# Down projections of the two MLPs: one 512-column stream past the high weights in place of two 256-column streams

## The chip, the cores and the metric

The kernel runs on one core of one Trainium2 chip. The metric is the device time of one execution in microseconds (us), as the median of several runs. TensorE (PE) does the matrix products, with a row of its own for weight loads (PEld); VectorE (DVE), ScalarE (ACT) and GpSimd (POOL) do the elementwise work; SyncE (SP) issues the weight transfers.

## The reference

A sequence of 256 tokens of width 1024 goes through two blocks of a first model (an mLSTM mixer with an MLP, then a gated short convolution with an MLP) and through one block of a second model (retention and pooling, cross attention over 256 memory rows, a gated feed-forward part, a last norm). The change touches the two MLPs of the first model alone:

```python
def sqrelu_mlp(x, w_up, w_down):        # 1024 -> 4096 -> 1024
    h = jax.nn.relu(x @ w_up)
    return (h * h) @ w_down

# in each of the two layers:
x = x + rms_norm(h, g[1])
h = sqrelu_mlp(rms_norm(x, g[2]), w_mlp_up[i], w_mlp_down[i])
x = x + rms_norm(h, g[3])
```

## The kernel before

Activations lie transposed in SBUF: 128 features per partition row, tokens along the free side (T = 256 columns). All weights reach the core as one sequence of slabs of 1 MB, each of 16 tiles of 128 x 128 (8 input chunks `k` by 2 output chunks `n`). SP loads slabs into four raw buffers. To keep the precision of fp32, each operand is split into a high part (rounded to fp32r) and a low part (the rest): ACT writes `wH` from `raw` (line 790), DVE writes `wL = raw - wH` (line 1230), each slab in two halves, into two buffers each. The `split` of slab b waits for PE to be done with slab b - 2.

For each tile PE does three products of 256 columns (`products`): high weights by high input (line 404), high weights by low input (405), low weights by high input (406). Each is a weight load and a matmul, so the high weights are loaded twice in a row. All three add up in the same 256 columns of a PSUM bank. A *triple* below is these three. Some phases (`slab_by_token`, lines 431 to 433) do the same with the operands the other way round.

A phase of the work is a run of slabs for one projection (`PHASES`, in program order, with the engine that drains each group's PSUM). Groups alternate between two PSUM tensors, `po0` and `po1`, each of two banks of 512 columns, of which 256 are used. A down projection (`down0`, `down1`) has 16 slabs in 4 groups of 4 slabs; each group gives 256 output features. Its input is the hidden activation in `hH` and `hL` (32 chunks of 256 columns each), written by ACT (line 983) and DVE (line 1491) in the up phase before it.

When a down group is done, ACT alone drains it (`keep_y`): a Square of the sum into `squares` (line 838) for the norm, then two Identity operations with the gain as scale into `y` (line 844). POOL adds up the squares of groups 0 to 2. After the last group PE goes on with a *filler*: a slab or two of work for the later cross attention (`f1` after layer 0, `f6` and `f3` after layer 1). Within the first filler slab, after chunk k = 1, PE takes the sums of squares (`norm_sums`, line 472), for which it waits for the last Square; after k = 4 it spreads the norm factors (`norm_spread`, line 479), for which it waits for DVE. DVE then scales y (line 1450), x is updated, and the next phase's inputs `xnH` and `xnL` are made; PE waits for these at the first slab of the next phase. The order on ACT at the end of a down phase is: first half of a weight split, Square, two Identities, second half of the split. That is the order in which the code is written; every engine takes its instructions in its own program order.

Of the kernel before, what the change touches and what calls it, by code (L numbers as in the profile page):

```python
# [9 lines left out]
P = 128  # L10
T = 256
# [3 lines left out]
F1 = 4 * D  # L15
# [17 lines left out]
HL = 2  # L33
# [1 line left out]

PHASES = [
# [6 lines left out]
    ("fup", 2 * F2 // 256, 2 * F2 // 256, "V"), ("fdown", F2 // P // 2, 4, "V"),  # L43
# [29 lines left out]
def build(nc, xT, memT, pos, weights, wgate, params, poolw, tri, mask, select, decay, freq, recount, out):  # L73
# [4 lines left out]
    with ctx:  # L78
        place = [nc.sbuf_base + (-nc.sbuf_base) % 64]

        def sb(name, shape, dt, at=None):
            size = int(np.prod(shape[1:])) * 4
            if at is None:
                off = place[0]
                place[0] += (size + 31) // 32 * 32
            else:
                off = at[0]
                at[0] += (size + 31) // 32 * 32
            return nc.alloc_sbuf_tensor_at(name, list(shape), dt, offset=off)

        def sem(name):
            return ctx.enter_context(nc.semaphore(name))
# [24 lines left out]
        at = [scratch]  # L117
# [19 lines left out]

        region = place[0]
        at = [region]
        hH = sb("hH", [P, F1 // P, T], f32r, at)  # L140
        hL = sb("hL", [P, F1 // P, T], f32r, at)
        hidden_end = at[0]

        cost = sb("cost", [P, T], f32, at)
# [121 lines left out]
        s_sum, s_ms, s_r, s_diag, s_R = sem("sumsq"), sem("mean_sq"), sem("r_ready"), sem("diag_ready"), sem("R_done")  # L266
        s_Rs = sem("R_kept")

        s_t, s_xadd, s_xaddV = sem("y_scaled"), sem("x_added_pool"), sem("x_added_dve")

        s_dch, s_ach, s_pch = sem("dve_chain"), sem("act_chain"), sem("pool_chain")
# [43 lines left out]
        def slot(g):  # L315
            return po[g % 2]
# [74 lines left out]
        def _(pe):  # L391
# [9 lines left out]
            def products(psum, n, w, k, aH, aL, ac, start, stop):  # L401
# [3 lines left out]
                pe.matmul(psum[:, n, 0:T], wH[w][:, wc], aL[:, ac, :], start=False, stop=False)  # L405
                return pe.matmul(psum[:, n, 0:T], wL[w][:, wc], aH[:, ac, :], start=False, stop=stop)  # L406

            def slab(s, w, psum, aH, aL, c0=0, first=True, last=True, ready=None, between={}):

                for k in range(8):  # L410
                    if k % 4 == 0:
                        weights_ready(s, k // 4)
                    if ready and k % 2 == 0:
                        pe.wait_ge(ready[0], ready[1] + k // 2 + 1)
                    for n in range(2):
                        mm = products(psum, n, w, k, aH, aL, c0 + k, first and k == 0, last and k == 7)
                    if k == 3:
                        mm.then_inc(s_half, 1)
                    if k in between:
                        between[k]()  # L420
                mm.then_inc(s_slab, 1)
# [170 lines left out]
            def mlp(layer, feed, n_norm, names):  # L592
                up, down = f"up{layer}", f"down{layer}"
                s0, g0 = SLAB0[up], GROUP0[up]
                d0 = DRAIN[g0][1]

                for j in range(4):
                    phase_slab(up, j, xnH, xnL, ready=(s_xn, 4 * feed) if j == 0 else None,
                               between=norm(n_norm) if j == 1 else {})
                with pe.Fori(0, 3) as i:  # L600
                    for j in range(4):

                        pe.wait_ge(s_drain["V"], i * 4 + (d0 + 4 + j - 2))
                        slab(i * 4 + (s0 + 4 + j), (s0 + j) % HL, slot(g0 + j), xnH, xnL)

                s0, g0 = SLAB0[down], GROUP0[down]
                d0 = DRAIN[g0][1]
                with pe.Fori(0, 2) as i:
                    for j in range(2):

                        slot_free(g0 + j)
                        pe.wait_ge(s_drain["A"], i * 2 + (d0 + j - 2))
                        for kk in range(4):
                            b = s0 + 4 * j + kk
                            slab(i * 8 + b, b % HL, slot(g0 + j), hH, hL, c0=8 * kk, first=kk == 0, last=kk == 3,
                                 ready=(s_hid, 16 * layer + 4 * kk) if j == 0 else None)
                fillers(names, n_norm + 1)

# [156 lines left out]
        def _(act):  # L775
# [60 lines left out]
            def keep_y(psum, g, gain):  # L836
# [7 lines left out]
                    k = act.activation(dst, psum[:, e, 0:T], ACT.Identity, scale=by)  # L844
                k.then_inc(s_drain["A"], 1)

            def mix_hi(src, pair, done):
                act.wait_ge(*done)
                act.activation(mixH[:, 2 * pair:2 * pair + 2, :], src, ACT.Copy).then_inc(s_mixH, 1)
# [120 lines left out]
            def mlp(layer, gain, n_norm):  # L970
                up, down = f"up{layer}", f"down{layer}"
                s0 = SLAB0[up]
                d0 = DRAIN[GROUP0[up]][1]

                def square(n, i=None):

                    def at(v, m=4):
                        return v if i is None else i * m + v
                    act.wait_ge(s_drain["V"], at(d0 + n))
                    act.activation(hsq[n % 2][:, :, :], hrelu[n % 2][:, :, :], ACT.Square).then_inc(s_hs, 1)  # L980
                    act.wait_ge(s_hs, at(16 * layer + n + 1))
                    dst = hH[:, 2 * n:2 * n + 2, :] if i is None else hH[:, bass.ts(i * 4 + n, 2), :]
                    act.activation(dst, hsq[n % 2][:, :, :], ACT.Copy).then_inc(s_hidH, 1)

                for n in range(4):
                    split(s0 + n + 2)
                    if n == 0:
                        keep_R(n_norm, Rs[:, :])
                    square(n)
                with act.Fori(0, 3) as i:  # L990
                    for j in range(4):
                        split(s0 + 4 + j + 2, i, 4)
                        square(4 + j, i)
                if layer == 1:

                    act.wait_ge(s_trig, 1)
                    act.activation(sint[:, :], ang[:, :], ACT.Sin).then_inc(s_trigd, 1)
                    act.activation(cost[:, :], turn[:, :], ACT.Sin).then_inc(s_trigd, 1)
                    act.wait_ge(s_trigd, 2)
                s0 = SLAB0[down]  # L1000
                with act.Fori(0, 2) as i:
                    for j in range(2):
                        for kk in range(4):
                            b = s0 + 4 * j + kk
                            split(b + 2, i, 8, halves=(0,))
                            if kk == 3:
                                act.wait_ge(s_slab, i * 8 + (b + 1))
                                keep_y(slot(GROUP0[down] + j), i * 2 + j, gain)
                            split(b + 2, i, 8, halves=(1,))

            out_phase("out0", "g01")
            boundary("f4", 0, "g02", 0)
# [201 lines left out]
        def _(dve):  # L1214
# [217 lines left out]
            def boundary(n, post, filler, feeds, gain, key):  # L1432

                nxt = SLAB0[filler] + 1
                two = nxt == SLAB0[f"f{key}"]
                split(nxt, halves=(0,))
                mean_square(n)
                if two:
                    split(nxt, halves=(1,))
                    diagonal(n)  # L1440
                    split(nxt + 1, halves=(0,))
                else:
                    diagonal(n)
                    split(nxt, halves=(1,))

                dve.wait_ge(s_R, n + 1)

                def scale(p):
                    ys = y[:, 2 * p:2 * p + 2, :]
                    dve.tensor_tensor(ys, ys, over_pair(pn[:, 128:128 + T]), ALU.mult).then_inc(s_t, 1)  # L1450

                def add(p):
                    dve.wait_ge(s_t, 4 * post + p + 1)
                    xs, ys = x[:, 2 * p:2 * p + 2, :], y[:, 2 * p:2 * p + 2, :]
                    dve.tensor_tensor(xs, xs, ys, ALU.add).then_inc(s_xaddV, 1)

                scale(0)
                add(0)
                scale(1)
                scale(2)  # L1460
                feed_pair(feeds, 0, gain)
                scale(3)
                add(2)
                if two:
                    split(nxt + 1, halves=(1,))
                for p in (1, 2, 3):
                    feed_pair(feeds, p, gain)
                fill_keys(key)
                split(nxt + 2 if two else nxt + 1)

            def out_phase(name):
                for i in range(3):
# [10 lines left out]
            def mlp(layer, n_norm):  # L1483
# [27 lines left out]
                s0 = SLAB0[down]  # L1511
                for kk in range(3):
                    split(s0 + kk + 2)
                with dve.Fori(0, 3) as i:
                    for kk in range(4):
                        split(s0 + 3 + kk + 2, i, 4)

            out_phase("out0")
            boundary(2, 0, "f4", 1, "g02", 0)
# [481 lines left out]
```

## Time and profile before

| | |
|---|---|
| Runs of the kernel before | 992.37, 995.93, 1000.08 us; median 995.93 |
| The profiled execution's own time | 998.9 us |
| Its span, first to last instruction | 996.5 us |
| Mean granted TensorE clock | 0.994 of full |
| Matmuls | 8062, each with a weight load |

Times of single instructions come from the profiled execution, whose span is 2.4 us less than its time. Matmuls overlap in the records: each lasts 0.28 us from start to modelled end, and the next one starts long before that end. The time that a matmul costs is therefore the distance from its start to the start of the next one (its *slot* below), not its length.

### The profile page before, as it was taken

How to read it: one execution, taken by the hardware profiler on the slowest of the kernel's cores; microseconds unless marked ns; L12 is line 12 of the kernel's file. 1: busy time of each engine (PE TensorE's matmuls, PEld its weight loads, DVE VectorE, ACT ScalarE, POOL GpSimd, SP SyncE). 2: the span in 40 equal slices, each digit the busy share in tenths (PEclk: the TensorE clock that was granted, in tenths of full speed). 3: DMA queues.
4: the chain of work that ended last, by engine and by line, in shares of the span. 5: the costliest groups of instructions: out<-in, count | busy, mean ns of one | idle time of the engine just before them, and what ended most of it. 6: DMA issues, size and time to landing. Idle time of an engine off the chain costs nothing.

```text
span 996.5 us, 20181 instructions
## 1 busy us (share of the span) xinstructions
PE 960.1 (96%) x8062; PEld 946.0 (95%) x8062; DVE 660.3 (66%) x843; ACT 534.8 (54%) x754; POOL 186.4 (19%) x159
## 2 busy tenths in 40 slices
PE   8999989999999899989999999889999999999995
PEld 7999989999999799989999999889999999999995
DVE  6667586665444877678665444774775779999642
ACT  5566646654444545556655443545554566666541
POOL 2121140000000400149100010455120122222101
PEclk9999999999999999999999999999999999999998
DMA  8533635555555355535655554544443545555521
GB/s 341 191 127 120 218 127 192 191 174 206 173 197 180 112 197 199 179 129 201 211 179 201 207 174 154 205 145 164 139 158 105 178 142 179 200 181 198 210 87 43
DMA packets 25844, 172.17 MB, mean 173 GB/s; under 512 B 3252, under 2 KB 3892, under 8 KB 5432
## 3 DMA queue, kind: packets, MB, share of 16 engines
q1 hardware_dynamic: 25784, 171.30, 49.5%
q8 instruction: 46, 0.75, 0.3%
q14 instruction: 14, 0.11, 0.0%
HBM read 170.24 MB, written 1.05 MB: 172 GB/s over the span
## 4 chain that ended last, share of the span: by engine, by line
PE 63%; DVE 15%; issue 6%; POOL 2%; ACT 2%; DVEq 1%; ACTq 0%; POOLq 0%
PE po L404 19%; PE po L405 19%; PE po L406 19%; DVE wL L1230 7%; DVE xnL L1237 2%; POOL rtok L1806 2%; DVE cval L1741 1%; DVE cgate L1741 1%; DVE apad L1728 1%; ACT wH L790 1%; PE po L432 1%; PE po L433 1%; PE po L431 1%; PE pn L479 1%; PE pc L728 1%
## 5 line engine op out<-in xcount | busy, mean ns | idle before, releaser
L1230 DVE TENSOR_TENSOR wL<-raw,wH 128x1024 fp32r<-128x1024 f32 x318 | 411.7, 1318 | 157.7 <-ACT wH L790 157.3
L790 ACT ACTIVATE wH<-raw 128x1024 fp32r<-128x1024 f32 x318 | 332.3, 1057 | 255.7 <-PE po L406 226.7
L404 PE MATMUL po<-xnH,wH 128*128 128x256 f32 x1376 | 391.4, 284 | 18.9 <-DVE xnL L1237 13.4
L405 PE MATMUL po<-xnL,wH 128*128 128x256 f32 x1376 | 383.6, 279 | 0.0
L406 PE MATMUL po<-xnH,wL 128*128 128x256 f32 x1376 | 383.4, 279 | 0.0
L404 PEld LDWEIGHTS po<-xnH,wH 128*128 128x128 f32 x1376 | 259.2, 188 | 24.3 <-DVE xnL L1237 10.3
L405 PEld LDWEIGHTS po<-xnL,wH 128*128 128x128 f32 x1376 | 260.5, 189 | 0.2
L406 PEld LDWEIGHTS po<-xnH,wL 128*128 128x128 f32 x1376 | 260.0, 189 | 0.0
L404 PE MATMUL po<-hH,wH 128*128 128x256 f32 x688 | 191.4, 278 | 1.3 <-DVE wL L1230 1.3
L405 PE MATMUL po<-hL,wH 128*128 128x256 f32 x688 | 191.3, 278 | 0.0
L406 PE MATMUL po<-hH,wL 128*128 128x256 f32 x688 | 191.3, 278 | 0.0
L1793 POOL TENSOR_TENSOR squares<-squares 128x512 f32<-128x512 f32 x26 | 39.7, 1526 | 515.9 <-ACT squares L838 362.1
L404 PEld LDWEIGHTS po<-hH,wH 128*128 128x128 f32 x688 | 129.1, 188 | 1.5 <-DVE wL L1230 1.5
L405 PEld LDWEIGHTS po<-hL,wH 128*128 128x128 f32 x688 | 130.2, 189 | 0.0
L406 PEld LDWEIGHTS po<-hH,wL 128*128 128x128 f32 x688 | 129.3, 188 | 0.0
L404 PE MATMUL po<-mixH,wH 128*128 128x256 f32 x256 | 71.8, 281 | 1.0 <-DVE mixL L1272 1.0
L405 PE MATMUL po<-mixL,wH 128*128 128x256 f32 x256 | 71.0, 277 | 0.0
L406 PE MATMUL po<-mixH,wL 128*128 128x256 f32 x256 | 71.0, 277 | 0.0
L1497 DVE SCALAR_TENSOR_TENSOR hrelu<-po,Rs 128x512 f32<-128x512 f32 x32 | 22.1, 691 | 49.2 <-PE po L406 49.0
L1237 DVE SCALAR_TENSOR_TENSOR xnL<-x,par,xnH 128x256 fp32r<-128x256 f32 x56 | 48.5, 918 | 7.4 <-ACT xnH L804 7.4
L404 PEld LDWEIGHTS po<-mixH,wH 128*128 128x128 f32 x256 | 48.1, 188 | 1.5 <-DVE mixL L1272 1.4
L405 PEld LDWEIGHTS po<-mixL,wH 128*128 128x128 f32 x256 | 48.3, 189 | 0.0
(284 smaller groups left out, 1083.8 us busy)
## 6 DMA issues: line engine op xcount, KB each, us to landing
raw<-in_weights SPq DMA_DIRECT2D x158, 1024.0 KB, 4.8
x<-in_xT SPq DMA_DIRECT2D x4, 256.0 KB, 5.7
raw<-in_weights SPq DMA_DIRECT2D x2, 512.0 KB, 5.5
mem<-in_memT SPq DMA_DIRECT2D x1, 1024.0 KB, 13.1
out<-y SPq DMA_DIRECT2D x4, 256.0 KB, 2.4
decayt<-in_decay SPq DMA_DIRECT2D x1, 512.0 KB, 3.7
poolwt<-in_poolw SPq DMA_DIRECT2D x1, 256.0 KB, 3.6
par<-in_params SPq DMA_DIRECT2D x1, 164.0 KB, 3.4
```

The lines of the kernel that those rows point to most:

```text
L404: pe.matmul(psum[:, n, 0:T], wH[w][:, wc], aH[:, ac, :], start=start, stop=False)
L405: pe.matmul(psum[:, n, 0:T], wH[w][:, wc], aL[:, ac, :], start=False, stop=False)
L406: return pe.matmul(psum[:, n, 0:T], wL[w][:, wc], aH[:, ac, :], start=False, stop=stop)
L431: pe.matmul(psum[:, t, 0:256], aH[:, k, tc], wH[w][:, wc], start=k == 0, stop=False)
L432: pe.matmul(psum[:, t, 0:256], aL[:, k, tc], wH[w][:, wc], start=False, stop=False)
L790: act.activation(wH[b % HL][:, hs], raw[b % RAW][:, hs], ACT.Copy).then_inc(s_hi, 1)
L1230: dve.tensor_tensor(wL[b % HL][:, hs], raw[b % RAW][:, hs], wH[b % HL][:, hs].bitcast(f32), ALU.subtract)\
L1237: k = dve.scalar_tensor_tensor(xnL[:, c, :], x[:, c, :], col(gain, c), xnH[:, c, :].bitcast(f32), ALU.mult, ALU.subtract)
L1497: dve.scalar_tensor_tensor(hrelu[n % 2][:, :, :], slot(GROUP0[up] + n)[:, :, 0:T], 0.0, over_pair(Rs[:, :]), ALU.max, ALU.mult).then_inc(s ...
L1741: k = dve.scalar_tensor_tensor(c, apad[n % 2][:, e, tap:tap + T], w, c, ALU.mult, ALU.add)
L1793: pool.tensor_tensor(sq[0], sq[0], sq[p], ALU.add).then_inc(s_sqa, 1)
L1806: pool.tensor_tensor(r[:, :], ms[:, :], minus_half[:, 0:TT], ALU.pow).then_inc(s_r, 1)
```

## The change

`hH` and `hL` become two views of one tensor `hX`, in which the 256 high and the 256 low columns of a chunk lie side by side. In the down phases, PE streams the 512 columns past one load of the high weights into all 512 columns of the bank (the high product lands in columns 0 to 255, the low one in 256 to 511), and then the 256 high columns past the low weights into columns 0 to 255. A triple becomes a *pair* of a wide and a narrow matmul. The two sums are joined when the group is drained: ACT copies the low part from PSUM to `y` (`keep_low_part`), DVE adds the high part to it (`add_parts`), and ACT then makes the Square and the two Identities from `y` (`gain_y`). The drain of the down groups counts as DVE's (`"V"` in `PHASES`). The last group's `add_parts` stands in DVE's `boundary`, ahead of `mean_square`. Loops over the down phase on ACT and DVE are written out.

```diff
-    ... ("down0", 16, 4, "A"), ... ("down1", 16, 4, "A"), ...
+    ... ("down0", 16, 4, "V"), ... ("down1", 16, 4, "V"), ...
-        hH = sb("hH", [P, F1 // P, T], f32r, at)
-        hL = sb("hL", [P, F1 // P, T], f32r, at)
+        hX = sb("hX", [P, F1 // P, 2, T], f32r, at)
+        hH, hL = hX[:, :, 0, :], hX[:, :, 1, :]
+        s_ylo, s_ygain = sem("y_low_part_kept"), sem("y_gained")
+            def wide_products(psum, n, w, k, aX, ac, start, stop):
+                wc = slice(k * 256 + n * P, k * 256 + (n + 1) * P)
+                pe.matmul(psum[:, n, :], wH[w][:, wc], aX[:, ac, :, :].rearrange("p a t -> p (a t)"), start=start, stop=False)
+                return pe.matmul(psum[:, n, 0:T], wL[w][:, wc], aX[:, ac, 0, :], start=False, stop=stop)
 ...
                     for n in range(2):
-                        mm = products(psum, n, w, k, aH, aL, c0 + k, first and k == 0, last and k == 7)
+                        if aL is None:
+                            mm = wide_products(psum, n, w, k, aH, c0 + k, first and k == 0, last and k == 7)
+                        else:
+                            mm = products(psum, n, w, k, aH, aL, c0 + k, first and k == 0, last and k == 7)
 ...
-                        pe.wait_ge(s_drain["A"], i * 2 + (d0 + j - 2))
+                        pe.wait_ge(s_drain["V"], i * 2 + (d0 + j - 2))
-                            slab(i * 8 + b, b % HL, slot(g0 + j), hH, hL, ...
+                            slab(i * 8 + b, b % HL, slot(g0 + j), hX, None, ...
 ...   (ACT)
+            def keep_low_part(name, g, layer):
+                act.wait_ge(s_slab, SLAB0[name] + 4 * g + 4)
+                act.activation(y[:, 2 * g:2 * g + 2, :], slot(GROUP0[name] + g)[:, :, T:2 * T], ACT.Copy).then_inc(s_ylo, 1)
+            def gain_y(name, g, gain, layer):
+                act.wait_ge(s_drain["V"], DRAIN[GROUP0[name] + g][1])
+                act.activation(squares[:, g, :, :], y[:, 2 * g:2 * g + 2, :], ACT.Square).then_inc(s_sq, 1)
+                act.wait_ge(s_sq, 4 * (4 * layer + 4) + g + 1)
+                for e in range(2):
+                    dst = y[:, 2 * g + e, :]
+                    k = act.activation(dst, dst, ACT.Identity, scale=col(gain, 2 * g + e))
+                k.then_inc(s_ygain, 1)
 ...
-                with act.Fori(0, 2) as i:
-                    for j in range(2):
-                        for kk in range(4):
-                            b = s0 + 4 * j + kk
-                            split(b + 2, i, 8, halves=(0,))
-                            if kk == 3:
-                                act.wait_ge(s_slab, i * 8 + (b + 1))
-                                keep_y(slot(GROUP0[down] + j), i * 2 + j, gain)
-                            split(b + 2, i, 8, halves=(1,))
+                for j in range(4):
+                    for kk in range(3):
+                        split(SLAB0[down] + 4 * j + kk + 2)
+                    split(SLAB0[down] + 4 * j + 5, halves=(0,))
+                    keep_low_part(down, j, layer)
+                    split(SLAB0[down] + 4 * j + 5, halves=(1,))
+                    gain_y(down, j, gain, layer)
 ...   (DVE, boundary)
                 split(nxt, halves=(0,))
+                if post % 2:
+                    add_parts(f"down{post // 2}", 3, post // 2)
                 mean_square(n)
 ...
                 dve.wait_ge(s_R, n + 1)
+                if post % 2:
+                    dve.wait_ge(s_ygain, 2 * post + 2)
 ...
+            def add_parts(name, g, layer):
+                dve.wait_ge(s_ylo, 4 * layer + g + 1)
+                ys = y[:, 2 * g:2 * g + 2, :]
+                dve.tensor_tensor(ys, ys, slot(GROUP0[name] + g)[:, :, 0:T], ALU.add).then_inc(s_drain["V"], 1)
 ...   (DVE, mlp)
-                with dve.Fori(0, 3) as i:
-                    for kk in range(4):
-                        split(s0 + 3 + kk + 2, i, 4)
+                for j in range(3):
+                    split(s0 + 4 * j + 5, halves=(0,))
+                    add_parts(down, j, layer)
+                    split(s0 + 4 * j + 5, halves=(1,))
+                    for kk in range(3):
+                        split(s0 + 4 * j + kk + 6)
```

## Rows read from the trace of the kernel before

**Rows 1.** The page, busy time by engine, and the granted clock by slice

```profile
PE 960.1 (96%) x8062; PEld 946.0 (95%) x8062; DVE 660.3 (66%) x843; ACT 534.8 (54%) x754; POOL 186.4 (19%) x159
...
PEclk9999999999999999999999999999999999999998
```

**Rows 2.** Tile hH in down0: count, duration ns, first and last start

```profile
L404 PE MATMUL po<-hH,wH x256: 281/281/281, 230.5 to 320.6; 128*128 128x256 f32 x128
```

**Rows 3.** The tile hH in down1

```profile
L404 PE MATMUL po<-hH,wH x256: 276/276/276, 528.5 to 615.2; 128*128 128x256 f32 x128
```

**Rows 4.** Windows in down0, down1: length, busy (x count) by engine, clock

```profile
264.00:320.80 56.80, 56.80 (x485) 56.80 (x484) 24.93 (x21) 23.62 (x26) 3.33 (x3) 1.00 0.55 186
536.00:600.00 64.00, 64.00 (x567) 64.00 (x566) 29.30 (x24) 28.62 (x33) 3.33 (x3) 1.00 0.54 183
```

**Rows 5.** PE timeline after down0: start us, length us, line, idle before

```profile
320.87 0.28 PE L406 MATMUL po<-hH,wL 128*128 128x256 f32 x1
...
322.40 1.40 PE L472 MATMUL pn<-ones,squares 128*128 128x1 f32 x12
323.66 0.36 PE L404 MATMUL po<-memH,wH 128*128 128x256 f32 x1
323.86 0.28 PE L405 MATMUL po<-memL,wH 128*128 128x256 f32 x1
...
328.31 0.28 PE L406 MATMUL po<-memH,wL 128*128 128x256 f32 x1
330.69 0.36 PE L404 MATMUL po<-xnH,wH 128*128 128x256 f32 x1 [2.10 <-DVE xnL L1237]
```

**Rows 6.** PE timeline: eight 256-column fp32 matmuls, then fp32r ones

```profile
741.90 1.89 PE L706 MATMUL pa<-memk,xq 128*128 128x256 f32 x8
743.44 0.47 PE L404 MATMUL po<-xnH,wH 128*128 128x256 f32 x1
743.75 0.28 PE L405 MATMUL po<-xnL,wH 128*128 128x256 f32 x1
743.87 0.28 PE L406 MATMUL po<-xnH,wL 128*128 128x256 f32 x1
```

**Rows 7.** ACT timeline at the end of down0

```profile
321.29 0.60 ACT L838 ACTIVATE squares<-po 128x512 f32 x1 [1.87 <-PE po L406]
321.79 0.83 ACT L844 ACTIVATE y<-po,par 128x256 f32 x2
322.50 1.06 ACT L790 ACTIVATE wH<-raw 128x1024 fp32r<-128x1024 f32 x1
```

**Rows 8.** DVE timeline at the end of down0

```profile
319.45 1.23 DVE L1230 TENSOR_TENSOR wL<-raw,wH 128x1024 fp32r<-128x1024 f32 x1 [1.54 <-ACT wH L790]
323.83 0.16 DVE L1250 TENSOR_SCALAR ms<-pn 128x2 f32<-128x2 f32 x1 [3.16 <-PE pn L472]
324.82 0.48 DVE L1256 TENSOR_SCALAR diag<-ident,rtok 128x128 f32<-128x128 f32 x2 [0.82 <-POOL rtok L1806]
...
326.51 0.69 DVE L1450 TENSOR_TENSOR y<-y,pn 128x512 f32<-128x512 f32 x1
```

**Rows 9.** ACT timeline at the end of down1

```profile
615.84 0.60 ACT L838 ACTIVATE squares<-po 128x512 f32 x1 [1.76 <-PE po L406]
616.34 0.84 ACT L844 ACTIVATE y<-po,par 128x256 f32 x2
617.05 1.07 ACT L790 ACTIVATE wH<-raw 128x1024 fp32r<-128x1024 f32 x1
```

**Rows 10.** PE timeline in the first filler slab after down1

```profile
616.90 1.39 PE L472 MATMUL pn<-ones,squares 128*128 128x1 f32 x12
```

**Rows 11.** Windows in up0, the convolution input phase and fup

```profile
160.00:230.00 70.00, 70.00 (x597) 70.00 (x596) 43.53 (x50) 40.38 (x49) 0.00 (x0) 1.00 0.55 184
370.00:430.00 60.00, 59.76 (x524) 59.43 (x524) 39.09 (x48) 31.52 (x42) 4.95 (x4) 1.00 0.55 192
890.00:940.00 50.00, 48.65 (x415) 48.45 (x414) 44.97 (x58) 28.65 (x39) 10.38 (x8) 1.00 0.55 190
```

More of the change, by code:

```diff
@@ L611, in mlp @@
                         slot_free(g0 + j)
-                        pe.wait_ge(s_drain["A"], i * 2 + (d0 + j - 2))
+                        pe.wait_ge(s_drain["V"], i * 2 + (d0 + j - 2))
                         for kk in range(4):
                             b = s0 + 4 * j + kk
-                            slab(i * 8 + b, b % HL, slot(g0 + j), hH, hL, c0=8 * kk, first=kk == 0, last=kk == 3,
+                            slab(i * 8 + b, b % HL, slot(g0 + j), hX, None, c0=8 * kk, first=kk == 0, last=kk == 3,
                                  ready=(s_hid, 16 * layer + 4 * kk) if j == 0 else None)
@@ L999, in mlp @@
                     act.wait_ge(s_trigd, 2)
-                s0 = SLAB0[down]
-                with act.Fori(0, 2) as i:
-                    for j in range(2):
-                        for kk in range(4):
-                            b = s0 + 4 * j + kk
-                            split(b + 2, i, 8, halves=(0,))
-                            if kk == 3:
-                                act.wait_ge(s_slab, i * 8 + (b + 1))
-                                keep_y(slot(GROUP0[down] + j), i * 2 + j, gain)
-                            split(b + 2, i, 8, halves=(1,))
+                for j in range(4):
[5 more added lines that the diff above has]
+                    gain_y(down, j, gain, layer)
             out_phase("out0", "g01")
```

4 rows, old and new, of the table PHASES are left out of this document.

## The prediction

> **What bounds the kernel now.** I read the page first. PE is busy for 96% of the span and the weight loads for 95%, DVE for 66%, ACT for 54% [rows 1]. The granted clock is at its full level in all slices but the first, which says 9 [rows 1]. So the kernel is one stream of load and matmul, and what counts is the slot from one start to the next. Next I read the tile view of hH. It has 256 matmuls of line 404 in each down phase, one per triple. In down0 they start from 230.5 to 320.6 us, 90.1 / 255 = 353.3 ns per triple or 117.8 per matmul [rows 2]. In down1 they start from 528.5 to 615.2, 86.7 / 255 = 340.0 ns per triple or 113.3 per matmul [rows 3]. The reader is to see that the same instructions run in two cadences, both at a granted clock of 1.00 and with PE busy all the time [rows 4]. It is not the clock, DVE or a DMA that makes the difference; the trace doesn't say what does. I call them the slow and the quick cadence. At 2.4 GHz the 256 columns are 107 ns of either slot.
>
> Third, what is a slot made of? Two rows price its parts. The norm sums of line 472 stream a single column past each load. From 322.40 to 323.86 lie twelve of them and one narrow matmul; less 0.12 for that, it is 1.34 / 12 = 112 ns each [rows 5]. So a load alone sets a pace of 112 ns, close to a slot with 256 columns: load and stream are almost balanced, and each slot pays a little more than either. The fp32 matmuls of line 706 stream for about twice as long past each load. From 741.90 to 743.75 lie eight of them and one narrow one; the narrow slot after it is 743.87 - 743.75 = 0.12, so the eight take 1.73 us, or 216 ns each [rows 6]. (At a change of data type the first start is recorded early, therefore I count across it.) There a long stream hides its load wholly.
>
> **The change on PE.** It removes one load in three and keeps all columns. A wide matmul is priced by rows 6 at 216 ns. The narrow one behind it is priced from both sides: 113 by the quick cadence [rows 3], 118 by the slow one [rows 2]. I take 118, since right after the long streams the slot is 0.12 [rows 6]. A pair is then 216 + 118 = 334 ns. In down0 that saves 353.3 - 334 = 19.3 ns x 256 = 4.9 us, in down1 340 - 334 = 6 ns x 256 = 1.5 us, together 6.4. With 113 for the narrow one it would be 2 x 256 x 5 ns = 2.6 us more, 9.0. The upper bound on a wide matmul is two slots of today, 227 to 236; then nothing is saved.
>
> The Trainium skill's page "TensorE: Matmul & The Clock Gate", section "Back-to-back issue gap", has a rule that speaks against the change: it gives 262 cycles for 256 columns and 518 for 512. By it two narrow ones cost only 6 cycles more than a wide one; that would be an estimated 2.5 ns x 512 = 1.3 us, less than the drain below costs. The trace disagrees on the first figure: 262 cycles would be 109 ns, and the rows show 113 and 118 [rows 2, 3]. On the second it agrees, with 216 ns [rows 6].
>
> **The drain within the down phase.** Groups 0 to 2 get an ACT Copy, a DVE add, a Square and two Identities in place of the Square and the Identities. The new Copy and add are bounded by rows of their size, 0.60 us from PSUM on ACT [rows 7] and 0.69 on DVE with one operand in PSUM [rows 8]. A group lasts 4 slabs, 64 pairs or 21 us, and PE needs a slot back only one group later. In 56.8 us of down0 DVE is busy for 24.9 and ACT for 23.6, in 64 us of down1 29.3 and 28.6 [rows 4]. ACT's second half of a split comes sooner after the end of a group than now, because only the Copy stands ahead of it where the Square and both Identities stood. `gain_y` makes ACT wait for DVE's add; behind that wait are the next weight splits, which aren't ready before PE is half through the next slab, 2.7 us on. Cost: nothing. If that cover were gone, each of six joins would cost up to 0.7 us. The unrolled loops, the new layout of hX (same elements, with gaps of 1 KB) and the DMA traffic (0.55 of capacity [rows 4]) I put at zero as well, from below too: none of them shortens anything on PE.
>
> **The drain of the last group.** Here the cover is gone. PE does only two chunks of the filler, and then `norm_sums` waits for the last Square. Now the Square starts at 321.29, 0.42 after the last down matmul's start, and ends at 321.89, while PE comes to the sums at 322.40 [rows 5, 7]. So there is half a microsecond of slack. After the change ACT does, from 321.29 on: the Copy; then, 0.50 later (as the Identities follow the Square at 321.79 [rows 7]), the second half of the split, for which its slab is already done. In its place the next operation would follow about 0.96 later (a 1.06 us operation with the overlap of 0.10 that the Square shows). DVE has been idle since 320.68 [rows 8] and adds from about 321.95 to 322.64, so the split covers the add. The Square starts at 321.29 + 0.50 + 0.96 = 322.75 and ends at 323.35. With 0.1 for the signal the sums start at 323.5 in place of 322.40: PE stands for 1.1 us. For down1 the same: 615.84 [rows 9] + 1.46 + 0.60 + 0.1 = 618.0 against 616.90 [rows 10], again 1.1. From below, if ACT were free for the Square as soon as the add is done, it would be 1.0; from above, with 0.2 of lag at each of the three hand-overs, 1.5. Can a later slack swallow this? No: the chain from the sums over ms (323.83), diag (324.82) and the scaling (326.51) to the first xnL is what the next phase waits for, 2.10 us at 330.69 [rows 5, 8]. It starts with the sums, so all of it moves back by the same amount. The Identities end some 0.9 after the Square, far ahead of the scaling. The cost is 2 x 1.15 = 2.3 us. What is late next is still xnL.
>
> **The sum.** 998.9 - 6.4 + 2.3 = 994.8 us against the profiled execution, a gain of 4.1. That execution is 0.3% above the median, 995.93, and the three runs span 7.7 us. A stay of some 1,700 matmuls in the other cadence (4.5 ns each) would make such a spread, so I take it for the noise of this kernel. Carried over to the median: 995.9 - 4.1 = 991.8.
>
> **The rivals.**
> - *Narrow slots in the quick cadence* (113 ns): 2.6 us less, 989.2. For it: down1 keeps that cadence for all of its 87 us [rows 3]. Against it: rows 6. Chance 0.15.
> - *The stream costs more than its columns, a wide matmul takes two slots*: nothing saved, 2.3 lost, 998.2. Against it: 216 ns in rows 6, though that is another data type. Chance 0.08. By the skill's rule above it would come out at almost the same place, 1.0 us above the time before.
> - *Slower: the change throws other phases into the slow cadence.* A cadence seems to be taken up when PE restarts and then stays: up0 runs at 70 / 0.1178, some 595 matmuls, the convolution phase at close to 113 ns (524 in 60 us), fup at the slow one again [rows 11]. The change shifts every restart behind it. Up1 and the input and output phases of the convolution have some 1,500 matmuls in the quick cadence; 4.5 ns each are 6.9 us. From 4.1 / 4.5 ns = 910 matmuls on, the gain is gone. With all of the 1,500 the time is 991.8 + 6.9 = 998.7, with as many again in the last part of the kernel 1005.6. For it: the cadence after down1 may be the slow one from now on. Against it: it is as likely to fall the other way. Chance 0.12.
> - *Other phases fall into the quick cadence*: up0 alone, 768 matmuls, gives 3.5 us, 988.3; with fup as well (1,056) 983.6. Chance 0.10.
> - *The load's pace of 112 ns holds for wide matmuls too*, so that a pair costs some 230: 256 x (123 + 110) = 60 us less, 934. Against it stand the eight at 216. Chance 0.01. The same section of the skill's page gives 131 ns per matmul for a sustained stream of 512 columns; no row here shows anything like it.
>
> **How the numbers follow.** The forecast, 991.8, has a chance of 0.54; its own range with the noise of a median of few runs is 988 to 996. Outside of 983 to 1000 lie the further half of the slow case (0.06), the one at 934 and a part of the quick one (0.05 together), and some noise (0.05). A difference under 1% is about what a measurement of this kernel can't tell from no change; for more than 1% the time has to be under 986 or over 1006. Faster: most of what falls below 986 is a quick cadence in more than one other phase, 0.13. Slower: only the slow cadence almost everywhere, or a stall that I don't see, 0.06. Same: 0.81.
>
> **What would show it.** In the tile view of hX the 256 starts of the high product should be 334 ns apart in both layers, so each down phase lasts 85.4 us. The page should count 512 matmuls fewer, 7550. PE should wait at the norm sums for ACT's Square, 1.1 us, twice, and for xnL as long as before. In between, no wait of PE for wL or a drain. The forecast is wrong if the pair is not 330 to 338 ns, if the wait at the sums is not near 1.1 us, or if the sum of the other phases moves by more than 4 us.

## The result

| | before | changed |
|---|---|---|
| Median of 15 runs each | 996.13 us (992.37 to 1002.86) | 1007.05 us (1002.86 to 1009.46) |
| Ratio | | 1.0091, 95% interval 1.0066 to 1.0116 |
| The profiled execution | 998.9, span 996.5 | 1004.25, span 1002.0 |
| Matmuls | 8062 | 7550 |

The change makes the kernel slower, by a little under one per cent. 991.8 was forecast, with a range up to 1000. The ratios here and below leave out runs that took over 1.5% longer than the fastest of the same kernel: none of these thirty, but three of the twelve of e1 (1012 to 1014 us) and three of the 29 of the kernel before beside it, which the medians given there still hold.

The page of the changed kernel, with busy time by engine, the granted clock by slice, and the two groups of the pair:

```profile
PE 964.1 (96%) x7550; PEld 925.7 (92%) x7550; DVE 664.5 (66%) x851; ACT 539.8 (54%) x762; POOL 198.7 (20%) x159
...
PEclk9999999999999999999999999999999999999998
...
L412 PE MATMUL po<-hX,wH 128*128 128x512 f32 x512 | 181.0, 397 | 0.0
...
L413 PE MATMUL po<-hX,wL 128*128 128x256 f32 x512 | 143.9, 281 | 0.0
```

There are 512 matmuls fewer, as forecast. Loads are busy for 92% in place of 95% [rows 1], but PE isn't done sooner: 964.1 us in place of 960.1. A share of load time went away that nobody was waiting for. PE's timeline in the middle of down0, the changed kernel:

```profile
280.00 0.40 PE L412 MATMUL po<-hX,wH 128*128 128x512 f32 x1
280.24 0.28 PE L413 MATMUL po<-hX,wL 128*128 128x256 f32 x1
280.35 0.40 PE L412 MATMUL po<-hX,wH 128*128 128x512 f32 x1
```

From wide to narrow it is 0.24 us, from narrow to wide 0.11 to 0.12. The starts in the trace are 235 and 118 ns apart: 353 a pair, what a triple cost in the slow cadence. The tile view of hX confirms it for each of the two phases (first and last start, 90.1 / 255 = 353.3 ns in both):

```profile
L412 PE MATMUL po<-hX,wH x256: 388/397/398, 228.4 to 318.5; 128*128 128x512 f32 x128
L412 PE MATMUL po<-hX,wH x256: 388/397/398, 528.9 to 619.0; 128*128 128x512 f32 x128
```

So down0 costs what it did [rows 2], down1 3.4 us more than in the profile before [rows 3]. The second place is the end of the down phases. PE, ACT and DVE after down0 in the changed kernel, three timelines:

```profile
318.75 0.28 PE L413 MATMUL po<-hX,wL 128*128 128x256 f32 x1
...
321.27 1.47 PE L482 MATMUL pn<-ones,squares 128*128 128x1 f32 x12 [0.83 <-ACT squares L864]
...
323.90 0.41 PE L405 MATMUL po<-memH,wH 128*128 128x256 f32 x1
...
331.09 0.36 PE L405 MATMUL po<-xnH,wH 128*128 128x256 f32 x1 [2.06 <-DVE xnL L1258]
```

```profile
319.07 0.60 ACT L860 ACTIVATE y<-po 128x512 f32<-128x512 f32 x1 [1.71 <-PE po L413]
319.56 1.05 ACT L800 ACTIVATE wH<-raw 128x1024 fp32r<-128x1024 f32 x1
320.51 0.62 ACT L864 ACTIVATE squares<-y 128x512 f32<-128x512 f32 x1
```

```profile
319.70 0.69 DVE L1500 TENSOR_TENSOR y<-y,po 128x512 f32<-128x512 f32 x1 [1.08 <-ACT y L860]
322.78 0.16 DVE L1271 TENSOR_SCALAR ms<-pn 128x2 f32<-128x2 f32 x1 [2.39 <-PE pn L482]
```

Copy, split and Square follow each other on ACT as forecast, the add lies under the split, and the sums start 2.52 us after the last down matmul (1.53 before [rows 5]). The new thing is further on: at 323.90 the matmuls are 0.41 us long and some 0.21 apart. The windows (length, busy time, then the granted clock as the first number after POOL's count) show the clock:

```profile
319.00:324.00 5.00, 4.17 (x35) 3.99 (x34) 1.09 (x4) 2.97 (x5) 0.71 (x1) 0.95 0.23 92
324.00:327.00 3.00, 3.00 (x16) 3.00 (x16) 1.47 (x4) 0.00 (x0) 0.00 (x0) 0.51 0.27 38
327.00:331.00 4.00, 2.03 (x18) 1.83 (x16) 3.96 (x7) 2.13 (x5) 1.27 (x1) 1.00 0.58 233
```

For 3.4 us, from 323.5 on, PE runs at 1.2 in place of 2.4 GHz, and again at 623.9 behind down1. Before, the same stretch ran at full clock. From the last down matmul to the first of the next phase it is 331.09 - 318.75 = 12.34 us in place of 9.82, and behind down1 15.83 in place of 13.48. That makes 3.4 + 2.5 + 2.4 = 8.3 us more. The span grew by 5.5 only, since other phases ran quicker this time: up0 has 615 matmuls in the 70 us that held 597 before [rows 11], and the whole phase is some 3 us shorter.

### The profile page after: what moved, and what is told of

It reads as the page before. It is cut to its first block, busy times and chain, and to the rows that moved or that the text cites. A ratio compares the mean times of both kernels' runs of the same rounds, so it can differ in the third digit from the quotient of the medians.

```text
span 1002.0 us, 19087 instructions
## 1 busy us (share of the span) xinstructions
PE 964.1 (96%) x7550; PEld 925.7 (92%) x7550; DVE 664.5 (66%) x851; ACT 539.8 (54%) x762; POOL 198.7 (20%) x159
## 4 chain that ended last, share of the span: by engine, by line
PE 63%; DVE 16%; issue 5%; ACT 3%; POOL 2%; DVEq 1%; ACTq 0%; POOLq 0%
PE po L405 13%; PE po L407 13%; PE po L406 13%; PE po L412 12%; DVE wL L1251 7%; PE po L413 6%; DVE xnL L1258 2%; DVE cgate L1775 2%; POOL rtok L1840 1%; DVE apad L1762 1%; DVE cval L1775 1%; ACT wH L800 1%; PE po L441 1%; PE po L443 1%; PE po L442 1%
## 5 line engine op out<-in xcount | busy, mean ns | idle before, releaser
L1251 DVE TENSOR_TENSOR wL<-raw,wH 128x1024 fp32r<-128x1024 f32 x318 | 402.1, 1288 | 152.4 <-ACT wH L800 152.2
L412 PE MATMUL po<-hX,wH 128*128 128x512 f32 x512 | 181.0, 397 | 0.0
L413 PE MATMUL po<-hX,wL 128*128 128x256 f32 x512 | 143.9, 281 | 0.0
L412 PEld LDWEIGHTS po<-hX,wH 128*128 128x128 f32 x512 | 96.3, 188 | 23.7
L413 PEld LDWEIGHTS po<-hX,wL 128*128 128x128 f32 x512 | 96.1, 188 | 0.0
L405 PE MATMUL po<-hX,wH 128*128 128x256 f32 x176 | 48.9, 278 | 1.2 <-DVE wL L1251 1.2
L406 PE MATMUL po<-hX,wH 128*128 128x256 f32 x176 | 48.7, 277 | 0.0
L407 PE MATMUL po<-hX,wL 128*128 128x256 f32 x176 | 48.7, 277 | 0.0
```

Source lines behind the costliest of these rows:

```text
L405: pe.matmul(psum[:, n, 0:T], wH[w][:, wc], aH[:, ac, :], start=start, stop=False)
L412: pe.matmul(psum[:, n, :], wH[w][:, wc], aX[:, ac, :, :].rearrange("p a t -> p (a t)"), start=start, stop=False)
L413: return pe.matmul(psum[:, n, 0:T], wL[w][:, wc], aX[:, ac, 0, :], start=False, stop=stop)
L1251: dve.tensor_tensor(wL[b % HL][:, hs], raw[b % RAW][:, hs], wH[b % HL][:, hs].bitcast(f32), ALU.subtract)\
```

## The experiments

The theory after the result (theory 1): a wide fp32r matmul costs by its columns, more than they are worth at 2.4 GHz, and the drain costs by a wait and a fall of the clock. Rival 2: the drain is all of it. Rival 3: the wide stream puts other phases into the slow cadence.

**e1: narrow matmuls, new drain.**

```diff
-                pe.matmul(psum[:, n, :], wH[w][:, wc], aX[:, ac, :, :].rearrange(...), start=start, stop=False)
+                pe.matmul(psum[:, n, 0:T], wH[w][:, wc], aX[:, ac, 0, :], start=start, stop=False)
+                pe.matmul(psum[:, n, T:2 * T], wH[w][:, wc], aX[:, ac, 1, :], start=False, stop=False)
```

> The changed kernel with the wide matmul undone: three narrow matmuls with three loads again, the low product going to columns 256 to 511 of the bank, and the new drain kept. Theory 1 (the wide matmul is priced by its columns, 0.46 ns each, 235 ns for 512, so a pair always costs the 353 ns of a slow triple; the new drain costs some 2.5 us at the end of each down phase, most of it by a granted clock that falls to half for 3.4 us): the triple is back at 340 or 353 ns, whichever cadence the execution takes, both boundaries keep the wait at the norm sums (0.8 us) and the half clock; the median lies about 5 us over the kernel before and 2 to 5 under the changed one, 1001 to 1004. Rival 2 (all of the loss is the drain): the same time as the changed kernel, 1006 to 1008. Rival 3 (the wide stream throws later phases into the slow cadence): 5 us or more under the changed kernel, with slow stretches fewer than there.

Measured: 1002.88 us, 0.999 of the kernel before (0.9956 to 1.0025), which itself had a median of 1002.2 in its 29 runs this time. The tile view of e1 in down0 and down1:

```profile
L412 PE MATMUL po<-hX,wH x256: 281/281/281, 231.3 to 321.4; 128*128 128x256 f32 x128
L412 PE MATMUL po<-hX,wH x256: 276/276/276, 533.5 to 620.2; 128*128 128x256 f32 x128
```

353 ns per triple in the first, 340 in the second. The quick cadence is back, so it is the wide matmul that shuts it out, and not the new layout of hX, which e1 keeps. Both waits at the sums (0.9 us) and both falls of the clock are there with narrow matmuls too (325.3 and 625.7, 3.4 us each); the stretches are 12.44 and 15.63 us. The drain makes them alone. The window of the first fall:

```profile
325.40:328.70 3.30, 3.30 (x17) 3.30 (x17) 1.77 (x4) 0.00 (x0) 0.71 (x1) 0.50 0.00 0
```

The median fell into the expected place, but the one of before had moved as far, so it tells little: the interval, -4.4 to 2.5 us, allows at most 2.5 us for the drain, less than the 4.9 of the profiles.

**e2: wide matmul, old drain.**

```diff
-                    keep_low_part(down, j, layer)
-                    split(SLAB0[down] + 4 * j + 5, halves=(1,))
-                    gain_y(down, j, gain, layer)
+                    act.wait_ge(s_slab, SLAB0[down] + 4 * j + 4)
+                    keep_y(slot(GROUP0[down] + j), j, gain)
+                    split(SLAB0[down] + 4 * j + 5, halves=(1,))
```

> The changed kernel with the old drain: wide and narrow matmul as there, but ACT makes Square and Identities straight from columns 0 to 255 of the sum, so the low product of the down projections is left out of the result. Theory 1: pairs of 353 ns in both layers, no wait at the norm sums, no fall of the granted clock at the end of the down phases; 3 to 5 us over the kernel before (half of the time its down phases would have run at 340), 999 to 1001. Rival 2 (all of the loss is the drain): no more than the kernel before, 995 to 997. Rival 3 (the wide stream throws later phases into the slow cadence): still 7 to 9 us over it, 1003 to 1006.

Measured: 1003.34, a ratio of 1.0026 (0.9995 to 1.0057). The tile view, both phases at 353 ns a pair:

```profile
L412 PE MATMUL po<-hX,wH x256: 389/397/398, 231.3 to 321.4; 128*128 128x512 f32 x128
L412 PE MATMUL po<-hX,wH x256: 388/397/398, 531.5 to 621.6; 128*128 128x512 f32 x128
```

No wait at the sums, no fall of the clock behind either phase, stretches of 9.82 and 13.73 us. Both costs sit where theory 1 puts them. Their size in the median isn't shown: it lies above the 999 to 1001 expected, but so does the kernel before beside it, and the interval of -0.5 to 5.7 us takes in the 3 to 5 expected and no change as well. Rival 3 asked for 7 to 9 and is out at that size. A smaller effect isn't excluded. Outside of the two down phases, 1691 narrow slots are slow (117 to 119 ns) in the profile of the changed kernel, 2672 in e3 and 3997 in e2, against 2245 to 2638 in the four profiles with narrow matmuls (before, e1, e7, e8). At 4.5 ns a slot the three lie 10 us apart, so they can't show 2 us.

**e3: the changed kernel with the sums later.**

```diff
-                fill(names[0], {1: lambda: norm_sums(n_norm), 4: lambda: norm_spread(n_norm)})
+                # behind a down phase:
+                fill(names[0], {3: lambda: norm_sums(n_norm), 5: lambda: norm_spread(n_norm)})
```

> The changed kernel with the norm sums after chunk 3 and the spread after chunk 5 of the first filler behind a down phase (after chunks 1 and 4 now). Theory 1, with the half clock set off by what PE does at the sums (a wait of 0.8 us next to twelve one-column matmuls, in all 2.3 us with next to no columns): no wait at the sums, the granted clock stays at 1.00, the restart of the next phase comes 1 to 2 us earlier after each down phase; 2 to 4 us under the changed kernel, 1003 to 1005. Rival (the clock falls because of the wide stream or by chance at this place, not by the wait): the clock still falls, and the time stays within 1 us of the changed kernel.

Measured: 1006.36, ratio 1.0058 (1.0026 to 1.0089). PE after down0 in e3, timeline, and two windows:

```profile
320.88 0.28 PE L413 MATMUL po<-hX,wL 128*128 128x256 f32 x1
...
323.82 1.40 PE L482 MATMUL pn<-ones,squares 128*128 128x1 f32 x12
...
331.94 0.54 PE L405 MATMUL po<-xnH,wH 128*128 128x256 f32 x1 [3.04 <-DVE xnL L1261]
```

```profile
321.00:331.00 10.00, 7.87 (x66) 7.46 (x64) 5.58 (x10) 4.40 (x8) 1.85 (x2) 1.00 0.29 101
332.00:335.30 3.30, 2.83 (x12) 2.53 (x12) 3.30 (x4) 2.62 (x7) 2.83 (x2) 0.50 0.04 17
```

The wait at the sums is gone and the clock holds through the filler. The stretches are 11.06 and 14.39 us, 1.3 and 1.4 shorter than in the changed kernel. But behind layer 0 PE now waits 3.04 us for xnL in place of 2.06, and there the clock falls. I had said that it would stay at 1.00; that holds for the filler and for layer 1 alone. In time the gain is 0.3% by the two ratios, with intervals that overlap. The median is 0.7 us under the changed kernel's, which is where the rival had put it, and above the 1003 to 1005 expected. So the traces show that the wait brings the fall in the filler; the time doesn't show that it is worth anything over many runs.

**e8: the kernel before with a later Square**, so the delay without the new operations.

```diff
                     split(SLAB0[down] + 4 * j + 5, halves=(0,))
+                    if j == 3:
+                        split(SLAB0[down] + 4 * j + 5, halves=(1,))
                     act.wait_ge(s_slab, SLAB0[down] + 4 * j + 4)
                     keep_y(slot(GROUP0[down] + j), j, gain)
```

> The kernel before with one delay alone: after the last group of each down phase ACT does the second half of the weight split ahead of the Square, which is then 0.95 us later; no new operation. PE should wait some 0.5 us at the norm sums. If a wait next to the one-column matmuls is what makes the granted clock fall in the changed kernel, and 0.5 us are enough, it falls here too, for 3.4 us, and the stretch from the last down matmul to the next phase grows by 1.5 us or more (9.8 and 13.5 before); if not, the stretch grows by the 0.5 us alone and the clock stays at 1.00.

Measured: 995.04 in one run. PE waits 0.42 us at the sums after each down phase, the stretches are 10.43 and 14.15 us, 0.6 and 0.7 longer, and the clock is full through both fillers (it fell only at 325.2, as PE started on the next phase):

```profile
316.84 0.80 PE L472 MATMUL pn<-ones,squares 128*128 128x1 f32 x6 [0.42 <-ACT squares L838]
...
314.00:325.00 11.00, 8.68 (x74) 8.31 (x72) 6.48 (x12) 4.29 (x9) 1.97 (x2) 1.00 0.46 171
```

So a wait of 0.4 here costs itself and a little more, and no clock.

**e7: the kernel before once more.**

> The kernel before once more, for a second profiled execution of the same program. If the two cadences are taken up anew at each restart of PE, other phases than in the first profile run at 340 or 353 ns per triple, and the span moves by 4.5 ns for each matmul that changed sides. If the cadence belongs to the program (addresses, order), the pattern is the same as in the first profile. The chain behind the down phases is 9.8 us and 13.5 us long as there, within 0.3.

Measured: 1000.26, span 997.9. Down0 ran at 353 ns per triple, down1 at 340, as in the first profile, but elsewhere the pattern is another: of the narrow slots 3013 are 117 to 119 ns long and 4312 are 113 or 114, against 3275 and 4053 in the first. In e8 both down phases are quick (86.7 us each), and 2422 slots are slow. The same program takes up its cadences anew in each execution, 4.5 ns a slot: the 262 slots between the two profiles are worth 1.2 us, the 853 between e8 and the first 3.8. The stretches are 9.82 and 13.60 us. One more thing was not expected: the clock fell here too, for 6.8 us at 332.7, when PE started on the next phase.

**e4: widths of 384 and 448 columns.**

```diff
-                pe.matmul(psum[:, n, :], wH[w][:, wc], both, start=start, stop=False)
+                cols = 2 * T if start else (384, 448)[layer]
+                pe.matmul(psum[:, n, 0:cols], wH[w][:, wc], both[:, 0:cols], start=start, stop=False)
```

> The changed kernel with the wide matmul cut to 384 columns in layer 0 and to 448 in layer 1 (from the second chunk on, so 128 and 64 columns of the low product are left out). Theory 1 (the stream pays by the column, 0.46 ns, whatever the load): wide slots of 177 and 206 ns, the narrow one behind them 118. Rival A (a wide matmul pays its columns at 2.4 GHz and a fixed price of some 20 ns above them): 181 and 208, close to the first. Rival B (the wide matmul falls into two passes of 256, each with a slot of its own): 235 in both. Rival C (a step above some width): anything that isn't in proportion.

Measured: 990.09 in one run. The wide slots are 182 ns for 384 columns (148 of the 248 are 182, the rest mostly 181 and 183), and 200 to 206 for 448, 203 in the mean. The narrow ones stay at 117 to 118. PE's timeline in down0 and in down1 of e4:

```profile
270.38 0.34 PE L414 MATMUL po<-hX,wH 128*128 128x384 f32 x1
270.55 0.28 PE L415 MATMUL po<-hX,wL 128*128 128x256 f32 x1
270.67 0.34 PE L414 MATMUL po<-hX,wH 128*128 128x384 f32 x1
...
559.94 0.36 PE L414 MATMUL po<-hX,wH 128*128 128x448 f32 x1
560.14 0.28 PE L415 MATMUL po<-hX,wL 128*128 128x256 f32 x1
560.25 0.37 PE L414 MATMUL po<-hX,wH 128*128 128x448 f32 x1
```

It goes neither in strict proportion (177 and 206) nor in passes of 256 (235). Counted from the columns at 2.4 GHz the surplus is 22 ns at 384, 17 at 448, 22 at 512, and 7 or 11 at 256. There is a price above the columns that doesn't shrink when the load is hidden; its form I can't tell.

**e5: both matmuls wide; narrow before wide.**

```diff
+                if layer == 0:
+                    pe.matmul(psum[:, n, :], wH[w][:, wc], both, ...)
+                    return pe.matmul(psum[:, n, :], wL[w][:, wc], both, ...)
+                pe.matmul(psum[:, n, 0:T], wL[w][:, wc], aX[:, ac, 0, :], ...)
+                return pe.matmul(psum[:, n, :], wH[w][:, wc], both, ...)
```

> The changed kernel with two other forms. Layer 0: both matmuls wide (the low weights also stream all 512 columns, which adds the product of the two low parts, left out before). Layer 1: the narrow matmul first, then the wide one. Theory 1 (a wide fp32r stream costs 235 ns by itself): layer 0 pays 235 for each, 470 a pair; layer 1 pays 353 as before, whichever comes first. Rival (a wide slot costs more because of the narrow one in front of it, or because its load falls beside a short stream): in layer 0 the wide slots fall towards the 216 ns of the fp32 products, 432 a pair, and in layer 1 the pair changes too.

Measured: 1035.73 in one run. Layer 0: 231 ns for the first wide one and 236 for the second, 467 together, not 432. Layer 1: 118 and 235, in the other order. The wide slot hardly depends on its neighbour, by 4 ns at most. PE's timeline in down0 of e5:

```profile
299.72 0.39 PE L416 MATMUL po<-hX,wH 128*128 128x512 f32 x1
299.95 0.40 PE L417 MATMUL po<-hX,wL 128*128 128x512 f32 x1
300.19 0.39 PE L416 MATMUL po<-hX,wH 128*128 128x512 f32 x1
```

**e6: loads of 64 columns; bf16.**

```diff
+                if layer == 0:
+                    wc = slice(wc.start, wc.start + 64)
+                    pe.matmul(psum[0:64, n, :], wH[w][:, wc], both, ...)
+                    return pe.matmul(psum[0:64, n, 0:T], wL[w][:, wc], aX[:, ac, 0, :], ...)
+                pe.matmul(psum[:, n, :], bw, bx, ...)            # constant bf16 tiles
+                return pe.matmul(psum[:, n, 0:T], bw, bx[:, 0:T], ...)
```

> The changed kernel with two other kinds of pair in place of all but the first and the last of each group (so most of the down projections is left out of the result). Layer 0: the same fp32r streams of 512 and 256 columns past loads of 64 columns. Layer 1: streams of 512 and 256 bf16 columns past loads of 128, from constant tiles. Theory 1a (the surplus over 213 ns comes from reading an fp32r stream, whatever is loaded): layer 0 stays at 235, layer 1 comes to about 216 for the wide ones. Theory 1b (the load steals time from the stream): layer 0 falls to about 225, layer 1 as now or a little under. Rival (the surplus comes from writing 512 columns of PSUM): 235 in both.

Measured: 999.04 in one run. With half the load the fp32r pair is 229 and 117 ns: half of a load is worth 6 ns, and 16 of the surplus stay. In bf16 the surplus is gone: 216 and 109, 325 a pair. PE's timeline in down1 of e6:

```profile
559.84 0.38 PE L423 MATMUL po<-io 128*128 128x512 bf16 x1
560.05 0.27 PE L424 MATMUL po<-io 128*128 128x256 bf16 x1
560.16 0.38 PE L423 MATMUL po<-io 128*128 128x512 bf16 x1
```

Writing 512 columns of PSUM isn't what costs, since the bf16 stream writes them as well. Theories 1a and 1b each hold a part: the load takes some, the data type the most. But the data type changed for the weights too, and a bf16 load is recorded at 98 ns where an fp32r one is at 188; so this pair doesn't tell the reading of the stream from the loading.

**e9: the kernel before with down projections in bf16**, since e6 points there.

```diff
+                h, l = bfpart(wH[w], k // 4)[:, o:o + P], bfpart(wL[w], k // 4)[:, o:o + P]
+                pe.matmul(psum[:, n, 0:T], h, hHb[:, ac, 0:T], start=start, stop=False)
+                pe.matmul(psum[:, n, 0:T], h, hLb[:, ac, 0:T], start=False, stop=False)
+                return pe.matmul(psum[:, n, 0:T], l, hHb[:, ac, 0:T], start=False, stop=stop)
```

> The kernel before with the down projections alone in bf16: high and low parts of weights and hidden activation are rounded to bf16 (the first to fp32r elsewhere), three narrow products and three loads as before, the old drain. This changes the precision of the down projections, not what is computed. If the surplus of a slot over its columns comes from reading fp32r streams, all three slots fall to the 109 ns that the narrow bf16 matmuls showed, 328 ns a triple in both layers and in every execution, in place of 340 or 353: 3 to 6.5 us less per layer, 6 to 13 us under the kernel before, some 9 in the median. If instead the load of 128 columns sets the pace where every stream is narrow (112 ns behind one-column products), a triple costs 336 and the gain is 2 to 9 us. If the other phases take up the slow cadence more often because they start at other moments, the gain is smaller than its down phases show.

Measured: 991.23 us (990.17 to 992.73, 6 runs) against 1001.39 for the kernel before beside it, ratio 0.987 (0.983 to 0.991), 10 us less. It is the fastest of the three, at the price of the rounding to bf16: it is no like-for-like rival of the fp32r kernels. The tile view of down1, and the windows in both phases (60 us each; PE, then the loads):

```profile
L424 PE MATMUL po<-hHb,shortH x256: 272/273/283, 526.4 to 609.9; 128*128 128x256 bf16 x128
```

```profile
240.00:300.00 60.00, 60.00 (x552) 53.79 (x550) 28.42 (x23) 27.70 (x33) 3.26 (x3) 1.00 0.56 194
540.00:600.00 60.00, 60.00 (x552) 53.78 (x551) 28.42 (x23) 27.70 (x32) 3.27 (x3) 1.00 0.58 201
```

83.5 / 255 = 327.5 ns per triple, 109 a slot, the same in both phases. That is 6.6 us less per layer than a slow phase and 3.2 less than a quick one.

## Why the prediction was wrong

- **"A wide matmul is priced by rows 6 at 216 ns"** is the step that failed; a pair was to cost 334 ns and costs 353. I took the price from fp32 matmuls, which stream for as long but in another data type; an fp32r stream of 512 columns costs 235 (changed kernel, e2, e5), a bf16 one 216 (e6). The rival that a wide matmul takes two slots had the right size and got 0.08. The forecast itself named the flaw of its row and priced it too low.
- **The narrow slot behind it, 118 ns**: right, in every pair of the changed kernel.
- **The saving per phase**, 4.9 and 1.5 us: none and -3.4. What the rival didn't say is that the pair holds the slow price in both phases of every profile that has it in this order (changed kernel, e2, e3), while triples are often quick. Of the profiles with narrow matmuls (before, e1, e7, e8) down0 was quick in one of four and down1 in all four. By these shares the change loses some (0.25 + 1) x 3.4 = 4.3 us on PE, an estimate from no more than eight phases.
- **The drain within the phase costs nothing**: right, no wait of PE for a drain or for wL within the down phases.
- **The last drain, 1.1 us each**: right as far as the wait goes. Where the clock held in spite of the new drain (layer 0 of e4 and e6), the stretch was 10.8 us against 9.82 (11.0 in e5, whose last matmul is a wide one). What was missing is the clock: with the fall it is 12.3 to 12.4, another 1.5. Behind down1 the stretch is 14.7 without the fall (e5) and 15.6 to 15.8 with it. The term of 2.3 us came to 4.9 in the profile. The rows before held PE's wait of 2.10 us without a fall [rows 5], and I took the clock for safe. That profile was an unlucky one, though. Over all runs the mean granted clock is 0.9912 with the new drain (15 of the changed kernel, 12 of e1) and 0.9919 with the old one (40 of the kernel before, 12 of e2). One fall of 3.4 us lowers it by 0.0017, so a run with the new drain has 0.4 of a fall more, give or take as much, where the profile had two more. By the stretches a fall costs 0.9 to 1.5 us, so that is an estimated 0.5 us; with the 1.0 and 1.2 that the stretches grew without a fall, the drain comes to some 2.7, near to the 2.3 forecast.
- **The range** ended at 1000. The slow rival's mechanism, other phases in the slow cadence, isn't what happened in the profiled execution: there up0 went to the quick one, as the rival at 988.3 has it, and that is luck. That cadences are taken up anew was right, and the spread of the medians of the kernel before, 996 to 1002 from one series to the next, shows how little one series of few runs says here.
- **Two slips in the working**, neither of which bears on the forecast: the rival at 934 adds up to 938 (995.9 - 60 + 2.3), and the slice of the clock that stands out in rows 1 is the last, with an 8, not the first.

For the two profiled executions the account closes. 994.8 was forecast. The pair cost 9.8 us more than that (a saving of 6.4 became a loss of 3.4), the drain 2.6 more (4.9 for 2.3), and the other phases 2.8 less: 1004.4, with 1004.25 measured. So the wide matmul's price is by far the largest miss.

For the medians it doesn't close as well. 4.3 for the pair and 2.7 for the drain make 7.0 us; the ratio says 9.1, with an interval from 6.6 to 11.6. The experiments on one part each came out at -1.0 (e1) and 2.6 us (e2), which together fall short of the whole; e3, close to the changed kernel and in the same series as these two, came to 5.8. The signs and the places are shown by the traces; how many us each part is worth in the median is not.

What stays open: what an fp32r slot pays for above its columns (the stream's own reading, or something that its load holds up), what decides between 113 and 118 ns, and whether the wide form makes the slow cadence likelier in other phases.

## What to carry to other kernels

Price a matmul shape by a row of the same data type: here bf16 slots were within 3 per cent of their columns at 2.4 GHz, and fp32r slots 6 to 14 per cent longer. A load that is hidden behind a stream gives nothing back when it is removed; ask first whether the stream alone isn't already the bound. And where PE stands for a moment next to matmuls of one column, look at the granted clock behind it before a wait is priced at its own length.

## What the runs showed of the hardware

**Slots by shape**, all at a granted clock of 1.00: fp32r 256 columns 113 or 118 ns, 384 columns 182, 448 columns 203, 512 columns 235 (231 and 236 where both are wide, 229 with half a load); bf16 256 columns 109, 512 columns 216. The Trainium skill, "TensorE: Matmul & The Clock Gate", section "Back-to-back issue gap", gives 262 and 518 cycles for 256 and 512 columns (109 and 216 ns at 2.4 GHz), as the gap of an isolated matmul. The bf16 rows agree with both; the fp32r ones are 4 to 9 and 19 ns above. By this table two streams of 256 cost next to nothing more than one of 512, and that was right for this change (2 x 118 against 235 ns), though not in its figures.

**Two cadences of the same code.** Narrow fp32r slots come in runs of 113.3 or of 117.8 ns, up to 1,500 matmuls long. A run mostly ends where something else comes between: a wait, an fp32 product. Behind the twelve one-column matmuls of the norm sums, in the 34 places of the eleven profiles where PE came to them without a wait or with one of 0.4 us, the slow cadence followed each time (the last sums of the kernel, with half clock behind them, are left out). In the ten with a wait of 0.8 to 0.9 us it was the slow one five times and the quick one three times (layer 0 of the changed kernel, e4 and e6); twice the clock fell before a cadence could be read.

**The clock in the filler.** With the new drain PE waits 0.8 to 0.9 us in front of the one-column matmuls. That happened at ten places (changed kernel, e1, e4, e5, e6, two each), and the clock fell in the filler behind six of them. At the twelve places without this wait or with 0.4 us of it (before, e2, e3, e7, e8, e9) it never did. At the restart of the phase after layer 0 it fell in seven of the eleven profiles, of both sorts. The fall is thus a matter of chance that the wait makes likelier, not a rule.
